# Two sparse layers of 32 small experts: 32 slots instead of 64, and each expert's rows mixed straight into the tokens' sum

## The reference, cut to what matters

```python
for gi in range(MOE_GROUPS):
    e0 = gi * MOE_EPG
    wg = jnp.where(g_sel[:, None] == gi, w_grp, 0.0).astype(x.dtype)
    hg = (jax.nn.silu(jnp.einsum('td,edf->tef', xt, w_gate[e0:e0 + MOE_EPG]))
          * jnp.einsum('td,edf->tef', xt, w_up[e0:e0 + MOE_EPG]))
    y = y + jnp.einsum('tef,efd->td', hg * wg[..., None], w_down[e0:e0 + MOE_EPG])
```

## Time and profile before

| what | value |
|---|---|
| median of 3 runs | 2313.65 us (2313.26 to 2318.51) |
| the profiled execution | 2317.6 us, its span 2315.9 us |
| TensorE busy | 2153.6 us (93%) |
| VectorE / ScalarE busy | 812.1 us (35%) / 669.3 us (29%) |
| mean granted TensorE clock | 0.975 |
| HBM read | 605.11 MB, 262 GB/s over the span |
| expert loop of the first layer | from 154 us to 392 us of the span |
| expert loop of the second layer | from 611 us to 852 us of the span |

### The profile page before, as it was taken

One profiled execution on the slowest core, in us unless ns is written; L12 is line 12 of the kernel. 1 busy time (PEld: TensorE's weight loads), 2 busy tenths in 40 slices (PEclk: granted clock), 3 DMA queues, 4 the chain that ended last, 5 costly groups with the idle time before them and its releaser, 6 DMA issues.

```text
span 2315.9 us, 47748 instructions
## 1 busy us (share of the span) xinstructions
PE 2153.6 (93%) x19825; PEld 1642.6 (71%) x19825; DVE 812.1 (35%) x1483; ACT 669.3 (29%) x1151; POOL 70.3 (3%) x122
## 2 busy tenths in 40 slices
PE   7899898998998989898999998989999999999997
PEld 6675555977654559887999897876667676676775
DVE  5541112665411126974566688540000000000002
ACT  4422222463332234554333346420000000000002
POOL 0100000101000002000000200000000000000000
PEclk9999999998999999999999999999999999999999
DMA  6079999601799986333454642419999999999993
GB/s 233 22 279 418 418 419 346 169 1 34 313 420 418 419 315 176 115 128 127 146 182 152 190 164 87 145 38 330 391 371 393 378 378 399 369 377 398 369 386 123
DMA packets 196759, 610.08 MB, mean 263 GB/s; under 512 B 11472, under 2 KB 87072, under 8 KB 163728
## 3 DMA queue, kind: packets, MB, share of 16 engines
q1 hardware_dynamic: 190688, 590.84, 67.8%
q0 software_dynamic: 5248, 13.25, 2.5%
q10 hardware_dynamic: 560, 2.10, 0.2%
HBM read 605.11 MB, written 1.05 MB: 262 GB/s over the span
## 4 chain that ended last, share of the span: by engine, by line
PE 75%; DVE 11%; DMA 6%; ACT 3%; issue 3%; DVEq 1%; ACTq 0%; POOLq 0%
PE psum L2269 18%; PE psum L2274 12%; PE psum L2010 8%; PE psum L160 7%; PE psum L162 7%; PE psum L161 7%; DMA weight_ring<-in_moe_w_up_dram 6%; PE psum L2041 3%; DVE weight_ring_rounded L139 2%; PE psum L959 2%; ACT scores L993 1%; PE psum L2050 1%; PE psum L945 1%; PE psum L2777 1%; PE psum L2306 1%
## 5 line engine op out<-in xcount | busy, mean ns | idle before, releaser
L2269 PE MATMUL psum<-weight_ring,weights_high 128*32 128x512 f32 (+2 forms) x4608 | 478.1, 470 | 0.0
L2274 PE MATMUL psum<-weight_ring,weights_high 128*32 128x256 f32 (+1 forms) x2304 | 445.5, 346 | 0.0
L2274 PEld LDWEIGHTS psum<-weight_ring,weights_high 128*32 128x32 f32 x2304 | 242.7, 110 | 54.8 <-issue 1.0
L2010 PE MATMUL psum<-weight_ring,scores 128*64 128x256 f32 x1632 | 228.2, 395 | 39.8 <-issue 28.4
L2269 PEld LDWEIGHTS psum<-weight_ring,weights_high 128*32 128x32 f32 x4608 | 184.1, 110 | 85.1 <-issue 41.1
L2274 PE MATMUL psum<-weight_ring,xT_high 128*32 128x256 f32 x1056 | 232.2, 379 | 0.0
L2269 PE MATMUL psum<-weight_ring,xT_high 128*32 128x256 f32 (+1 forms) x2112 | 231.5, 486 | 0.0
L2010 PEld LDWEIGHTS psum<-weight_ring,scores 128*64 128x64 f32 x1632 | 130.4, 140 | 127.7 <-issue 88.8
L160 PE MATMUL psum<-xT_high_rounded,weights_high_rounded 128*128 128x256 f32 x768 | 216.8, 282 | 2.2 <-DVE xT_rounded L392 1.4
L162 PE MATMUL psum<-xT_high_rounded,weight_ring_rounded 128*128 128x256 f32 x768 | 216.2, 281 | 0.0
L2378 DVE TENSOR_TENSOR xT<-xT,psum 128x768 f32<-128x768 f32 (+1 forms) x24 | 21.8, 910 | 512.4 <-PE psum L2274 374.1
(11 more groups left out here) (582 smaller groups left out, 3277.1 us busy)
## 6 DMA issues: line engine op xcount, KB each, us to landing
weight_ring<-in_moe_w_down_dram SPq DMA_DIRECT2D x142, 1024.0 KB, 9.1
weight_ring<-in_moe_w_up_dram SPq DMA_DIRECT2D x116, 1024.0 KB, 9.7
weight_ring<-in_moe_w_gate_dram SPq DMA_DIRECT2D x114, 1024.0 KB, 10.3
weight_ring<-in_moe_w_gate_dram SPq DMA_DIRECT2D x32, 768.0 KB, 6.5
weight_ring<-in_moe_w_up_dram SPq DMA_DIRECT2D x32, 768.0 KB, 4.5
weight_ring<-in_w_in_dram SPq DMA_DIRECT2D x20, 1024.0 KB, 8.5
weights_high<-in_moe_w_gate_dram SPq DMA_DIRECT2D x14, 1024.0 KB, 14.9
weights_high<-in_moe_w_up_dram SPq DMA_DIRECT2D x12, 1024.0 KB, 13.0
```

What stands on the lines that cost most here:

```text
L2010: last = self.c.nc.tensor.matmul(psum[at:at + W, x % 2, 0:CH], self.x[:, x % 2, k, :], w[:, k, :], start=(k == 0), stop=(k == k1 - 1), ski ...
L2269: last = nc.tensor.matmul(psum[32 * q:32 * q + 32, bank + c0 // 512, 0:c1 - c0], slots(q), w[:, c0:c1], start=start, stop=stop, skip_group ...
L2274: last = nc.tensor.matmul(psum[96:P, bank + c0 // 512, at:at + rest], slots(q, True), w[:, main:], start=start and at == 0, stop=stop, ski ...
```

## The change

`SmallExperts` uses windows of 32 slots. Gate and up are each cut into two halves of 128 columns, so that four products stand side by side in four groups of 32 array columns. The down product is cut into four quarters of 256 columns. Instead of being turned and written to `outT`, the result rows (4 x 32 partitions) are multiplied with a per-expert spread matrix `S`, which holds the weights, and accumulate in PSUM banks 0 to 3 over all experts. `S` is made anew for each expert: VectorE compares slot numbers with the token's place (`choose`), TensorE turns it, VectorE copies it. The common stage after the experts is left out for these layers; it is moved into a function `mix_slots` that only the large experts call. Tiles are loaded in the order gate, up, down, and all three are released together, after the down product. An expert with more than 32 slots runs an additional arm for the rest. There is one branch per expert and engine, with the extra arm behind it.

```diff
-    W = 64
+    W = 32
...
         for k in range(k0, k1):
-            for w, at in ((up, 0), (gate, W)):
-                last = self.c.nc.tensor.matmul(psum[at:at + W, x % 2, 0:CH], self.x[:, x % 2, k, :], w[:, k, :],
+            for q, (w, m) in enumerate(((up, 0), (up, 1), (gate, 0), (gate, 1))):
+                last = self.c.nc.tensor.matmul(psum[q * W:(q + 1) * W, 4 + x % 2, 0:P], self.x[:, x % 2, k, :], w[:, k, m, :],
...
     def second(self, pe, x):
-        self.gate_and_up(x, KD // 2, KD).then_inc(self.c.ring.used, 2)
+        self.gate_and_up(x, KD // 2, KD).then_inc(self.gated.sem, 1)
...
+        transpose(psum[:, 6, 0:P], self.hidden_rows, self.c.ident[:, :])
+        for t in range(TT):
+            last = transpose(psum[:, 6, (1 + t) * P:(2 + t) * P], self.G[:, x % 2, t, :], self.c.ident[:, :])
...
+    def down(self, pe, x):
...
         for m in range(2):
+            for h in range(4):
+                last = self.c.nc.tensor.matmul(psum[h * W:(h + 1) * W, 7, 0:256], self.hidden[:, m, :], wt[:, m, h * 256:(h + 1) * 256],
+                                               start=(m == 0), stop=(m == 1))
+        last.then_inc(self.downed.sem, 1)
+
+    def mix(self, pe, x):
...
+        for t in range(TT):
+            for h in range(4):
+                last = self.c.nc.tensor.matmul(psum[:, h, t * 256:(t + 1) * 256], self.S[h * W:(h + 1) * W, x % 2, t, :],
+                                               self.rows[h * W:(h + 1) * W, x % 2, :], start=(x == 0 and t == 0), stop=(x == self.n - 1),
+                                               skip_group_check=True)
...
+    def release(self, x):
+        for sem, count in ((self.wide_pe.sem, self.each[self.wide_pe]), (self.c.ring.used, 3)):
+            self.c.nc.tensor.matmul(self.c.psum[0:self.W, 4 + x % 2, 256:257], self.c.ident[:, 0:self.W], self.c.ones[:, 0:1],
+                                    start=True, stop=True).then_inc(sem, count)
...
+    def tensor(self, pe):
         for x in range(-1, self.n):
             if x + 1 < self.n:
                 self.first(pe, x + 1)
             if x >= 0:
                 self.turn(pe, x)
+            if x >= 2:
+                self.mix(pe, x - 1)
+            if x + 1 < self.n:
+                self.second(pe, x + 1)
+            if x >= 0:
+                self.down(pe, x)
+                if x == 0:
+                    self.mix(pe, 0)
+                self.by_width(pe, x, lambda: self.release(x), lambda: self.wide(pe, x))
+        self.mix(pe, self.n - 1)
...
+        def choose(x):
+            if x >= 2:
+                dve.wait_ge(*self.of(self.turned, x - 2))
+            for t in range(TT):
+                last = nc.vector.tensor_scalar(self.G[:, x % 2, t, :].rearrange("p (q s) -> p q s", q=4), self.iota[:, 0:W].unsqueeze(1).broadcast_to([P, 4, W]),
+                                               self.pos[:, t, x:x + 1], self.weight[:, t, x:x + 1], ALU.is_equal, ALU.mult)
+            last.then_inc(self.chosen.sem, 1)
...
-        for s in range(SLOTS // P):
+        for s in range(0 if ahead else SLOTS // P):
...
+        if ahead:
+            dve.drain().then_inc(*matrices.up())
+            weights(dve)
+            nc.vector.tensor_tensor(pos[:, :, :], place[:, :, :], off[:, :].unsqueeze(1).broadcast_to([P, TT, n]), ALU.subtract)
+            dve.drain()
+            c.dve(nc.vector.tensor_tensor(prod[:, :, :, :], oh[:, :, :, :], pw[:, :, :].unsqueeze(3).broadcast_to([P, TT, 2, n]), ALU.mult))
+            c.dve(nc.vector.tensor_tensor(weight[:, :, :], prod[:, :, 0, :], prod[:, :, 1, :], ALU.add))
+            return
...
+    if not ahead:
+        mix_slots(c, outT, xg_rounded, spread, slot_w, mixed)
...
+            if ahead:
+                made, x = c.psum[:, 0:4, t * 256:(t + 1) * 256], c.x[:, t, :].rearrange("p (h n) -> p h n", h=4)
...
                 if ahead:
-                    load_once(p0, gate(0, 0))
-                    load_once(p0 + 1, up(0, 0))
                     for x in range(n):
...
+                        load_once(p0 + 3 * x, gate(x, 0))
+                        load_once(p0 + 3 * x + 1, up(x, 0))
+                        load_once(p0 + 3 * x + 2, down(x, 0))
```

More of the change, by code:

```diff
@@ L1974, in __init__ @@
[L1974 to L1976 removed]
+        self.hidden, self.primed = spare[:, 0:2 * W].rearrange("p (m s) -> p m s", m=2), spare[:, 256:258]
+        self.squashed_rows, self.hidden_rows = spare[0:2 * W, 512:640], spare[:, 640:768]
@@ L1981, in count, with of, load_count, by_width @@
             x.count += each * self.n
-    def of(self, signal, x, i, part=None):
+    def of(self, signal, x, part=None):
         each = self.each[signal]
[L1986 to L1994, removed]
+        return signal.sem, self.base[signal] + each * x + (each if part is None else part)
+    def load_count(self, eng, x):
+        return eng.value_load(self.cnt[0:1, bass.ds(x, 1)], min_val=0, max_val=TOK)
+    def by_width(self, eng, x, small, wide):
+        count = self.load_count(eng, x)
         with eng.If(count < self.W + 1):
@@ L2039, in third @@
         for m in range(2):
[L2040 to L2051, removed]
@@ L2060, in wide_first @@
                 for k in range(KD):
[L2061 to L2070, removed]
-        wt = self.c.ring.view(self.down_tile(x), 2, D)
[L2072 to L2077, removed]
@@ L2079, in tensor @@
-    def tensor(self, pe, sum_slots):
-        following = None
+                    nc.tensor.matmul(psum[:, bank, m * TOK:(m + 1) * TOK], wt[:, k, m, :], self.wide_x[:, k, :],
+                                     start=(k == 0), stop=(k == KD - 1))
+        for b in range(2):
+            for t in range(TT):
+                last = nc.tensor.transpose(psum[:, 7, (2 * b + t) * P:(2 * b + t + 1) * P], self.wide_G[:, t, b * P:(b + 1) * P], self.c.ident[:, :])
+        last.then_inc(self.wide_pe.sem, 1)
@@ L2081, in tensor @@
+        last.then_inc(self.c.ring.used, 3)
+    def tensor(self, pe):
         for x in range(-1, self.n):
-            count = following
-            if x == 0:
-                sum_slots(pe)
             if x + 1 < self.n:
-                following = self.load_count(pe, x + 1, 0)
                 self.first(pe, x + 1)
@@ L2166, in steps @@
-    def steps(self, eng, step, begin, end):
-        start = 2
-        turns = (self.n - 2 - start) // self.unroll
-        for x in range(begin, start):
-            step(eng, x, 0)
-        with eng.Fori(0, turns) as i:
-            for x in range(start, start + self.unroll):
-                step(eng, x, i)
-        for x in range(start + turns * self.unroll, end):
-            step(eng, x, 0)
-    def scalar(self, act, o):
-        self.steps(act, lambda eng, x, i: self.scalar_step(eng, x, i, o if x == -2 else None), -2, self.n)
```

648 lines of the change are left out of this document (333 added, 315 removed).

## The result

The change makes the kernel slower: 2409.35 us (2406.11 to 2411.35, 4 runs) against 2315.76 us (2313.26 to 2318.51, 4 runs) in the same comparison, a ratio of 1.0403 (95% interval 1.0383 to 1.0422). The forecast was 2289, with a range of 2274 to 2312.

The account below looks back on a forecast made before the run. Transfers were taken to bound the loop. Gains of 4.0 and 3.7 us (starts), 11.4 and 15.8 (tails), less 6.6 (fetch), 3 (clock) and 0.5 (next stage), gave 24.8 us: 2289 against the median, range 2274 to 2312.

Parts of the forecast that it names:

- instruction fetch: In the tails of the expert loops: one fetch pause of 3.3 us in each, 6.6 us lost in all.
- the third rival: In the loop: TensorE becomes the bound through fetch pauses at jumps, 8.5 us a turn, 39 us slower, 2353; chance 0.13.
- The loop bound by transfers, gain 0: In the expert loop: three tiles take 7.5 us to transfer, so a shorter TensorE turn gains 0.
- The turn, 4.8 us: One expert's TensorE work in the loop: 4.8 us after the change against 6.4 before.
- The mix, 1.1 us: Within each turn: 16 instructions of 256 columns in four row groups overlap and take 1.1 us.
- the second rival: In the mix: row groups do not run beside each other, 3.4 us instead of 1.1, total 2307; chance 0.10.
- The start: At each loop's start: shorter holes without transfers, gaining 4.0 us in the first layer and 3.7 in the second.
- The tail: From the last up tile to the adds' end: 12.5 us in the first layer; gains 11.4 and 15.8 us.
- The first rival: After the experts: the next stages' tiles come late, some 6 us per layer given back, 2301; chance 0.12.

Follow-up runs that it names:

- the four parts: The changed kernel with its full extra arm on TensorE cut into four parts, each behind a branch of its own: 2410.92 us (1.0413).
- quarter loads and no arm: The changed kernel without TensorE's branch and extra arm, loading only a quarter of each weight tile from each layer's fifth expert on: 2111.51 us (0.9121).
- quarter arm: The changed kernel with TensorE's extra arm cut to the gate product, 72 instructions with the release: 2285.42 us (0.9884).
- half arm: The changed kernel with TensorE's extra arm cut to the gate and up products, 136 instructions: 2333.06 us (1.0088).
- with one branch: The changed kernel with TensorE branching once per layer on the largest count, over a second copy of the loop: 2289.90 us (0.9896).
- with eight: The changed kernel with TensorE branching once per four experts, eight branches a layer, over a copy of those turns with arms: 2320.18 us (1.0036).

## Why the prediction was wrong

**The step that failed** is the one on instruction fetch: "I take one in each tail, 6.6 us in all", and in the third rival "most turns today have none, and TensorE would wait for the tile in that time anyway". I compared jumps (64 and 32 matmul instructions in two arms against 116 in one) and let today's rate of pauses stand, so the forecast had 6.6 us for fetch in the tails and nothing in the loops, where the arm cost 129. The quantity was instructions per turn against what the fetch delivers. The code jumped over grew little, from 192 to 232 by the count used above; the executed code grew from 92 to 206, and that was in no term. Before, 284 pass in 7.4 us; after, 438 would have to pass in 7.26, 60 per us, and about 47 come. The few pauses of the kernel before, worth 12 us, were the sign that it was near the limit, and the knee between 278 and 342 instructions is where it lies for a turn of 7.3 us. I gave this rival 0.13.

**The third rival** had the bound and its place right (instruction fetch, seen as "issue" before the expert's first product) and was sized too small: 8.5 us a turn and 2353. Its price was per jump, and the four parts show that it is not; that 3.3 per jump comes close to the measured 3.07 a turn is luck. The terms as measured: TensorE's own turn 4.58 (with start and tail), "issue" 196.5 / 64 = 3.07 (I had 3.3), and the lower clock: the eight groups of the expert lines are busy 476.7 us against 375.1 with quarter loads and no arm, 101.6 / 64 = 1.6 (I had 1.5 in the mean of those turns, but took 8.5 for the average over all). This last term is an estimate: it puts all of the longer busy time down to the clock. 4.58 + 3.07 + 1.6 = 9.25, against 9.17 measured. 64 x (9.17 - 7.26) = 122 us of the 129 that lie between the changed kernel with its arm and without. The other error is its base: I took 25 us of gain off, where 33.8 are there.

**The other steps,** read from the changed kernel without TensorE's arm, whose profiled span is 38.5 us shorter than before:

- The loop bound by transfers, gain 0: right, 419 to 420 GB/s and a turn of 7.26 us.
- The turn, 4.8 us: right (4.58). The mix, 1.1 us: 1.15, so the second rival (row groups not concurrent, 3.4) is refuted. The Trainium skill, TensorEngine Tiling (Array Packing), Key Properties, says that changing the tiling mode drains the engine; at the 0.2 us that I had put on each of two more changes the turn would be 5.2 us. No run here isolates such a drain, and that price is not borne out: the turn with all its changes of shape is shorter than my sum without a price for them.
- The start, 4.0 us in the first layer: without transfers from 152 to 173 are 12.0 us before and 7.0 without arms, 5.0 us. The first product started at 150.50 there, 1.5 us before the time in my sum.
- The tail, 12.5 us from the last up tile to the end of the adds: 373.51 to 385.28, 11.8 us:

```profile
373.51 1.13 PE L2016 MATMUL psum<-weight_ring,scores 128*32 128x128 f32 x32 [1.31 <-DMA weight_ring<-in_moe_w_up_dram]
...
381.48 1.15 PE L2060 MATMUL psum<-xT,xT_high 32*128 32x256 f32 x16 [0.52 <-ACT xT L2147]
...
382.93 2.35 DVE L2838 SCALAR_TENSOR_TENSOR x<-x,psum 128x1024 f32<-128x1024 f32 x2 [3.21 <-POOLq L248]
...
383.02 3.29 PE L153 MATMUL psum<-mask,ident 128*128 128x256 f32 x14 [0.40 <-POOLq L248]
```

- In the whole first layer 406.3 - 385.3 = 21.0 us are gained where I had 15.4. Of the rest 4.7 us are pauses of the kernel before: without its arms its adds start at 399.29 instead of 403.95.
- The first rival (late loads of the next stage) came true in one place, with another transfer than I named, and for a small part. After the second layer 44.3 us are gained at the adds (868.9 to 824.6), and 37.9 at the next stage's normalization (990.30 to 952.43). On the chain between stands a parameter load; before, it took 3.7 us and was there in time:

```profile
825.51 7.43 DMA cat<-in_norm_mix_w_dram
833.02 1.23 DVE scores L3056
```

VectorE waits 1.71 us for it. A larger part of the 6.4 us is the first group of products behind it, here and then in the kernel before:

```profile
839.38 6.58 PE L644 MATMUL psum<-probs_turned,scores 128*128 128x128 f32 x32 [9.25 <-DVEq L3064]
...
880.18 3.84 PE L644 MATMUL psum<-probs_turned,scores 128*128 128x128 f32 x32 [1.81 <-DVEq L3032]
```

It takes 2.7 us longer, at a granted clock of 0.55 in the mean from 837 to 846 (1.00 before, from 878 to 885), behind 9.25 us in which TensorE stood idle instead of 1.81.

## What to carry to other kernels

Count the instructions that pass an engine per turn, executed and jumped over, and divide by the turn: here some 47 per us came through beside transfers of 300 to 330 GB/s, and an arm that never ran cost 129 us. Beside fuller transfers there is less room: a quarter arm at 37.5 per us cost 5 us, a half arm at 42.9 cost 53. Put rare arms outside the loop, behind one branch, or keep them so short that the sum stays well under that; cutting one arm into several changed nothing. A change that halves the work per instruction (128 columns instead of 256) raises this load, here from 92 to 206 executed instructions, so a few scattered "issue" pauses in the kernel before are a price list and not noise.

## What was not expected of the hardware

- Never executed arms of up to 232 instructions were fetched whole, one 16 KB packet for about 250 instructions; jumps over 1750 or more skipped most of the fetch but left TensorE idle, for 5.2 us with one branch and 7 us per jump with eight.
- The fetch delivered 47 to 48 instructions per us beside transfers at 303 to 330 GB/s, 43 beside 377, and 58 beside 106 GB/s. What sets the rest of its pace stays open; no run here varies it.
- Behind one-column products (64 instructions in 10.57 us) the granted clock stood at its lower level, 1.2 GHz, though TensorE had been busy all the time. The sum of the slots' weights, which the change takes away, is such a stretch (157.64 to 162.6): the clock stood at 0.50 from 160 to 163.
